# Modulation sums as rows in column quarters, layer norm factors by tokens, and low-rank products spread over row groups

## The chip, the core and the metric

The kernel runs on one core of one Trainium2 chip. The metric is the device time of one execution in microseconds (us); smaller is better. Five engines work side by side, each with a queue of its own: TensorE (PE, matrix products into the PSUM banks), VectorE (DVE), ScalarE (ACT), GpSimd (POOL) and SyncE (SP, which here only issues transfers). They wait for each other by semaphores.

## What is computed

Two transformer-like blocks of two layers each work on 512 tokens of width 1024, all in float32. The first has a recurrent or a forgetting-attention mixer, cross-attention to 256 memory tokens and a squared-ReLU MLP. The second is the one that the change touches most:

```python
for l in range(DEPTH):                                   # second_block
    mod = c_act @ ada_w[l] + ada_b[l]                    # 6144 numbers: six vectors of 1024
    sh1, sc1, gt1, sh2, sc2, gt2 = [m[:, None, :] for m in jnp.split(mod, 6, axis=-1)]
    h = rms_norm_2(x, norm1_g[l]) * (1 + sc1) + sh1
    if l == 0:
        p = h @ w_in[0]; vl = None
    else:
        p = h @ jnp.concatenate([w_in[l], v_down[l - 1]], axis=1)
        vl = token_shift(p[..., N_IN:], mu_v[l - 1])     # 32 wide
    ps = token_shift(p[..., :N_SHIFT], mu_shift[l])      # r, k, v, wl (64), al (64), gl (160)
...
    log_w = -jax.nn.softplus(-(w0 + jnp.tanh(wl) @ w_up)) - 0.5
    a = jax.nn.sigmoid(a0 + al @ a_up)
    g = jax.nn.sigmoid(gl) @ g_up
    v = v + (v_first - v) * jax.nn.sigmoid(v0 + vl @ v_up)   # layer 1 only
```

Then come the delta-rule scan, a pooling branch (trailing means over 2, 4, 8 and 16 frames and a linear map), two gated projections, an output product and a gated MLP.

## The kernel before

**Tiles.** The activations stay in SBUF as `xT`, 8 tiles of 128 features by 512 tokens. Each weight arrives in slabs of 1024 x 256 (1 MB) through two buffers `raw`. ACT rounds a slab to `whi` (line 858) and DVE writes the rest `wlo` (line 1533), both in a two-place ring. A product with the split operands takes three float32r matmuls (lines 2393 to 2395): high by high, high by low, low by high. One block of 128 output features is 8 x 3 of them, and a slab has two blocks. A matmul with plain float32 operands appears in the trace as two instructions.

**Order.** Every engine's program is written out by hand. `Plan.walk` numbers all PSUM results ("jobs"). Job j uses bank j mod 8, and PE may start it only when job j - 8 has been read (`bank_read`). The vectors in small tables (`vec`) come from `vrows` by a transpose on PE.

**Modulation.** While the first block's two MLPs run, POOL loads `ada_w` and DVE sums it into `ada_acc` (128 partial sums for each of 6144 columns; lines 1967 and 1970). PE then adds up the 128 partitions: 48 products with a 128 x 128 piece of `ada_acc` as the stationary operand and one column of ones moving. For layer 0 these stand between the matmuls of a slab (`adaln_beside`, line 2612, slab `v`,0 of the first block's layer 1). For layer 1 they stand in a row (`adaln(1)`, line 2491), ahead of the first product `lat` of the second block. `adaln` on DVE (lines 1624 to 1634) puts the result into `mod` and derived tables.

**Front norms** (before `lat`, numbers 4 and 6 in the code). ACT squares the 8 tiles (line 888), DVE adds them up (1544, 1547), and PE multiplies by a matrix of 1/1024 (`mean_square`, 2474), which gives the mean square in all partitions. ACT takes the root of 128 x 512 (893) and DVE the reciprocal (1552). Then for each tile DVE scales (1566), ACT shifts and rounds to `hh` (900), and DVE makes `hl` (1573), on which `lat`'s matmuls wait tile by tile. For norm 6 (layer 1) the squares are made beside the last products of layer 0; for norm 4 they all come after the first block's last MLP product.

**Low-rank part.** After `lat` (two blocks: 64 + 64 features for wl and al, 128 of gl) comes `gl1` (a block with 32 useful features, the rest of gl), in layer 1 also `vl` (another block with 32), then the slab `k2`,0. Then PE makes `lw` (4 products of 64 rows, partitions 0 to 63; line 2779), `la` (4 of 64 rows, partitions 64 to 127; 2782) and in layer 1 `lv` (4 of 32 rows, all on partitions 0 to 31; 2787), then slab `k2`,1. ACT reads them by sigmoids (1260). A shifted result is made by ACT (1230, own share) and DVE (2018, the token before).

**Gates.** After the scan, PE makes for each t of 4 a product of 128 rows (3095) and one of 32 rows (3096, all on partitions 0 to 31) into one bank. DVE multiplies (2249), and ACT and DVE split the result. Then PE has the slab `g1` (48 matmuls) and four products `pool` (3109), each of which waits for POOL's window means of that tile (lines 806 to 815).

## Time and profile before

| | |
|---|---|
| median of 3 runs | 2894.18 us (2889.81 to 2898.56) |
| the profiled execution, its own time | 2896.48 us |
| its span in the trace | 2894.9 us |
| PE busy | 2758.8 us, 95% of the span |
| DVE, ACT, POOL busy | 1601.4, 987.7, 211.2 us |
| matmuls of lines 2393 to 2395 with `hh` and `mh` | 2040 + 1248 of each line |

In the profile a busy PE isn't always at full speed. The granted clock (PEclk) of a stretch tells which of two levels, 2.4 GHz (1.00) or 1.2 GHz (0.50), it had. A matmul shown as 0.39 us long starts 0.23 us after the one ahead of it at the full clock, and at half the clock 0.43 us after it. The chain of work that ended last says which instruction was waited for at each moment, so the times between the starts are what counts.

### The profile page before, as it was taken

The numbers are of one execution on the slowest core, as the hardware profiler recorded it, in microseconds if no ns is written. First come the engines' busy times: TensorE is split into PE (matmuls) and PEld (weight loads), VectorE is DVE, ScalarE is ACT, GpSimd is POOL, SyncE is SP. The second block draws the span as 40 slices with busy tenths as digits, with TensorE's granted clock in tenths as the row PEclk, the third lists the DMA queues.
The fourth block names the chain that finished last, engine by engine and source line by source line (L and its number), as shares of the span: only waits on it lengthen the run. The fifth ranks groups of instructions, "written<-read, shape, count | busy, mean of one in ns | idle before, by whom it ended". The sixth has DMA issues, their size and how long they took to land.

```text
span 2894.9 us, 45409 instructions
## 1 busy us (share of the span) xinstructions
PE 2758.8 (95%) x19273; PEld 2287.6 (79%) x19273; DVE 1601.4 (55%) x2301; ACT 987.7 (34%) x1352; POOL 211.2 (7%) x268
## 2 busy tenths in 40 slices
PE   8989999999999999998999999999878899999998
PEld 6778888898688888767868788888667868888887
DVE  5657777755677777564453553334485454543334
ACT  5643212334532122343333331223433333432223
POOL 4100000000000000001040000000020040000000
PEclk9999999999999999899999999999899999999999
DMA  4234555512045555120022323232210022323322
GB/s 152 90 107 128 182 167 166 165 59 73 17 140 178 171 166 171 55 74 25 4 78 88 102 88 102 91 99 82 73 59 12 3 87 89 101 90 100 101 89 72
DMA packets 238530, 281.94 MB, mean 97 GB/s; under 512 B 7444, under 2 KB 224856, under 8 KB 238344
## 3 DMA queue, kind: packets, MB, share of 16 engines
q1 hardware_dynamic: 225312, 227.07, 24.7%
q0 software_dynamic: 12896, 52.11, 6.1%
q8 instruction: 148, 2.42, 0.4%
q14 instruction: 38, 0.31, 0.0%
q10 hardware_dynamic: 136, 0.03, 0.0%
HBM read 277.09 MB, written 2.10 MB: 96 GB/s over the span
## 4 chain that ended last, share of the span: by engine, by line
PE 87%; DVE 7%; ACT 4%; issue 2%; DMA 1%; ACTq 0%; DVEq 0%; POOL 0%; POOLq 0%
PE psum L2393 24%; PE psum L2394 24%; PE psum L2395 24%; DVE wlo L1533 2%; PE psum L2452 1%; ACT whi L858 1%; PE psum L2894 1%; PE psum L2453 1%; PE psum L2454 1%; PE psum L2909 1%; PE psum L2491 1%; PE psum L2877 1%; PE psum L2824 1%; PE psum L3010 0%; PE psum L3016 0%
## 5 line engine op out<-in xcount | busy, mean ns | idle before, releaser
L1533 DVE TENSOR_TENSOR wlo<-raw,whi 128x2048 fp32r<-128x2048 f32 x222 | 520.7, 2346 | 529.7 <-ACT whi L858 529.4
L2393 PE MATMUL psum<-hh,whi 128*128 128x512 f32 (+1 forms) x2040 | 792.2, 388 | 19.6 <-DVE hl L1573 6.6
L2394 PE MATMUL psum<-hl,whi 128*128 128x512 f32 (+1 forms) x2040 | 785.5, 385 | 0.0
L2395 PE MATMUL psum<-hh,wlo 128*128 128x512 f32 (+1 forms) x2040 | 784.5, 385 | 0.0
L858 ACT ACTIVATE whi<-raw 128x2048 fp32r<-128x2048 f32 x222 | 423.9, 1909 | 558.7 <-PE psum L2395 554.6
L2393 PE MATMUL psum<-mh,whi 128*128 128x512 f32 (+1 forms) x1248 | 486.4, 390 | 3.1 <-issue 2.3
L2394 PE MATMUL psum<-ml,whi 128*128 128x512 f32 (+1 forms) x1248 | 480.1, 385 | 0.0
L2395 PE MATMUL psum<-mh,wlo 128*128 128x512 f32 (+1 forms) x1248 | 479.9, 385 | 0.0
L2393 PEld LDWEIGHTS psum<-hh,whi 128*128 128x128 f32 x2040 | 386.7, 190 | 109.1 <-issue 26.8
L2395 PEld LDWEIGHTS psum<-hh,wlo 128*128 128x128 f32 x2040 | 386.4, 189 | 76.1
L2394 PEld LDWEIGHTS psum<-hl,whi 128*128 128x128 f32 x2040 | 386.7, 190 | 74.6 <-issue 0.5
L2393 PEld LDWEIGHTS psum<-mh,whi 128*128 128x128 f32 x1248 | 235.7, 189 | 48.9 <-issue 4.5
L2395 PEld LDWEIGHTS psum<-mh,wlo 128*128 128x128 f32 x1248 | 235.4, 189 | 46.4
L2394 PEld LDWEIGHTS psum<-ml,whi 128*128 128x128 f32 x1248 | 235.5, 189 | 44.3 <-issue 0.5
L1970 DVE SCALAR_TENSOR_TENSOR rest<-rest,cact 128x192 f32<-128x192 f32 (+1 forms) x448 | 187.7, 419 | 15.8
L1677 DVE SCALAR_TENSOR_TENSOR xT<-psum,mod,xT 128x512 f32<-128x512 f32 x64 | 47.4, 750 | 156.5 <-PE psum L2395 156.5
L1211 ACT ACTIVATE mh<-rest 128x512 fp32r<-128x512 f32 x64 | 40.5, 633 | 253.1 <-DVE rest L1981 253.1
L798 POOL DMA_DIRECT2D rest<-in_ada_w x64 | 56.7, 887 | 922.7 <-DVE rest L1970 618.8
L1675 DVE TENSOR_TENSOR xT<-xT,psum 128x512 f32<-128x512 f32 x80 | 54.6, 685 | 110.2 <-PE psum L2395 110.2
L2340 DVE TENSOR_TENSOR rest<-rest,psum 128x512 f32<-128x512 f32 x40 | 27.5, 688 | 110.4 <-PE psum L2395 110.4
L1491 ACT ACTIVATE mh<-rest 128x512 fp32r<-128x512 f32 x44 | 27.8, 633 | 173.9 <-DVE rest L2340 172.5
L1484 ACT ACTIVATE rest<-psum 128x512 f32<-128x512 f32 x40 | 23.9, 598 | 143.3 <-PE psum L2395 143.2
(455 smaller groups left out, 2816.2 us busy)
## 6 DMA issues: line engine op xcount, KB each, us to landing
rest<-in_ada_w POOLq DMA_DIRECT2D x64, 768.0 KB, 5.3
raw<-in_w_gu SPq DMA_DIRECT2D x44, 1024.0 KB, 5.1
raw<-in_w_in SPq DMA_DIRECT2D x34, 1024.0 KB, 5.3
raw<-in_w_mlp_in SPq DMA_DIRECT2D x32, 1024.0 KB, 5.4
raw<-in_w_mlp_out SPq DMA_DIRECT2D x32, 1024.0 KB, 5.2
raw<-in_w_out SPq DMA_DIRECT2D x16, 1024.0 KB, 5.2
raw<-in_w_down SPq DMA_DIRECT2D x16, 1024.0 KB, 5.3
raw<-in_w_mem_kv SPq DMA_DIRECT2D x8, 1024.0 KB, 5.2
```

What stands on the lines that cost most here:

```text
L798: pool.dma_start(ada[:, s % 2, :, :], w[:, :, bass.ds(c * (per * ADA_COLS) + s * ADA_COLS, ADA_COLS)])\
L858: act.activation(whi[:, g % 2, :, :], raw[:, g % 2, :, :], ACT.Copy).then_inc(hi_done, 1)
L1211: act.activation(mh[:, m, :], f_t[:, m % 2, :], ACT.Square).then_inc(hid_hi, 1)
L1533: ins = dve.tensor_tensor(wlo[:, g % 2, :, :], raw[:, g % 2, :, :], f32(whi[:, g % 2, :, :]), ALU.subtract)
L1675: free(dve.tensor_tensor(xT[:, t, :], xT[:, t, :], bank(j), ALU.add), j)
L1677: free(dve.scalar_tensor_tensor(xT[:, t, :], bank(j), gate, xT[:, t, :], ALU.mult, ALU.add), j)
L1970: ins = dve.scalar_tensor_tensor(acc, w, cact[:, k:k + 1], acc, ALU.mult, ALU.add)
L2393: pe.matmul(out, whi_, xhi, start=first, stop=False)
L2394: pe.matmul(out, whi_, xlo, start=False, stop=False)
L2395: return pe.matmul(out, wlo_, xhi, start=False, stop=last)
L2452: pe.matmul(p[:, 0:n], xh[:, k, t], wh, start=(k == 0), stop=False)
L2453: pe.matmul(p[:, 0:n], xl[:, k, t], wh, start=False, stop=False)
```

## The change

- The modulation sums are turned round. `modulation_rows` makes three PSUM banks, each by four products: a column of ones, repeated 32 times, is stationary (128 x 32), and 512 columns of `ada_acc` move. Each product writes another quarter of the bank's partitions (32 equal rows). ACT copies a bank to SBUF (`modulation_row`, 128 x 512). `modulation_turned` brings the numbers from rows back to columns, by 4 products a bank with four columns of the identity matrix moving.
- For layer 0 the rows come after the slab `v`,0 and the turning after slab `k`,0, and nothing stands between the matmuls any more. For layer 1 the rows come right behind the last MLP product of the first block, ahead of the mean square. One bank is turned between the mean square and the factors, two behind the factors.
- The front norms take their mean squares by tokens (`mean_square_tokens`: 4 products of one column), root and reciprocal on 128 x 4, and spread the factor by 4 products with the identity (`factor_rows`). DVE's scaling reads it from PSUM. Norm 4's squares and sums move beside the last MLP products, as norm 6's already were.
- `gl1` and `vl` become one block. The 32 columns of the weights (and in layer 1 the 32 of `v_down`) are copied side by side four (two) times into 128 columns by the splitting itself (`latent_parts`), so that the 32 rows exist in every row group where they are wanted. The biases and loads of `mu_shift`, `mu_v`, `v_up` and `g_up` follow.
- `lw` and `la` alternate. `lv` runs on partitions 32 to 63 and 96 to 127 in turn. The four gate products of 128 rows come first, then the four of 32 rows, on four row groups in layer 0 and on two in layer 1.
- ACT takes a root of a small table at the start of the last `fd` slabs, which loads the function table there.

The diff, cut to its core:

```diff
@@ Plan.walk
                 self.slab_jobs("v", 1, 0, NT)
+                for r in range(3):
+                    self.add("mr", 0, r)
+                self.slab_jobs("k", 1, 0, NT)
                 self.add("mod", 0)
-                self.slab_jobs("k", 1, 0, NT)
...
-            if l:
-                self.lin("vl", l, 1, 1)
@@ vector (norm)
-                q.mark(dve.reciprocal(n_rstd, n_rs))
...
+                dve.reciprocal(tk[:, 1, :], tk[:, 0, :]).then_inc(S("front_factor"), 1)
+                j = J["rb", ni]
+                ready(dve, j)
+                norm_apply(ni, gain, shift, factor=bank(j))
@@ vector (last MLP chunk)
-                        if l == 0 and cc == CHUNKS1 - 1 and i >= 5:
-                            raw_lo(2, lambda t: V("norm_mix", 8 + t), (2 * i - 10, 2 * i - 9))
-                            norm_sums(2, range(max(1, 2 * i - 10), 2 * i - 8))
+                        if cc == CHUNKS1 - 1 and i >= 5:
+                            if l == 0:
+                                raw_lo(2, lambda t: V("norm_mix", 8 + t), (2 * i - 10, 2 * i - 9))
+                            norm_sums(2 + 2 * l, range(max(1, 2 * i - 10), 2 * i - 8))
@@ tensor
-                for n in range(48):
-                    ins = pe.matmul(p[:, n:n + 1], ada_acc[:, n * P:(n + 1) * P], ones[:, 0:1], start=True, stop=True)
+                for r in range(3):
+                    p = start("mr", l, r)
+                    for c in range(4):
+                        ins = pe.matmul(p[32 * c:32 * c + 32, :], ones[:, 0:1].to_broadcast([P, 32]),
+                                        ada_acc[:, (4 * r + c) * T:(4 * r + c + 1) * T], start=True, stop=True)
+                    done(ins)
...
+                evacuated(pe, J["mr", l, r])
+                for i in range(4):
+                    ins = pe.matmul(p[:, 16 * r + i:16 * r + 16:4], ada_rows[l][:, r, i * P:(i + 1) * P], ident[:, 0:P:32],
+                                    start=True, stop=True)
...
-                    linear_tokens("v", l, 0, h, NT, beside=adaln_beside)
...
+                    linear_tokens("v", l, 0, h, NT)
+                    modulation_rows(0)
...
-                mean_square(4 + 2 * l)
                 if l == 0:
-                    adaln(1)
+                    modulation_rows(1)
+                mean_square_tokens(4 + 2 * l)
+                if l == 0:
+                    modulation_turned(1, 0, ahead("mod", 1))
+                factor_rows(4 + 2 * l, l + 1)
...
                 linear("gl1", l, 0, h, blocks=1)
-                if l:
-                    linear("vl", l, 0, h, blocks=1)
...
-                        done(pe.matmul(p, VU[0:32, t * P:(t + 1) * P], VL[0:32, :], start=True, stop=True))
+                for t in range(4) if l else ():
+                    a = value_rows(t)
+                    p = start("lv", l, t)
+                    done(pe.matmul(p, VU[a, t * P:(t + 1) * P], GL[a, 1, :], start=True, stop=True))
...
+                p = [start("g", l, t) for t in range(4)]
                 for t in range(4):
-                    gate(t)
+                    pe.matmul(p[t], GU[:, 0, t * P:(t + 1) * P], GL[:, 0, :], start=True, stop=False)
+                for t in range(4):
+                    a = gate_rows(l, t)
+                    done(pe.matmul(p[t], GU[a, 1, t * P:(t + 1) * P], GL[a, 1, :], start=False, stop=True))
```

TensorE where the second block begins, before: the last MLP matmuls, then the mean square of norm 4, the 48 products of `adaln(1)`, then `lat`.

```order
4276 L2394 MATMUL psum<-ml,whi 128x512
4277 L2395 MATMUL psum<-mh,wlo 128x512
4278 L2474 MATMUL psum<-rest,mean_all 128x512
4279 L2491 MATMUL psum<-ones,rest 128x1 x48
4280 L2393 MATMUL psum<-hh,whi 128x512
```

The same place in the changed program (`rest` beside `ones` is `ada_acc`, beside `mean_all` the sum of squares, beside `ident` the copied rows; `tk` holds the factors).

```order
4254 L2452 MATMUL psum<-ml,whi 128x512
4255 L2453 MATMUL psum<-mh,wlo 128x512
4256 L2550 MATMUL psum<-rest,ones 32x512 x12
4257 L2567 MATMUL psum<-mean_all,rest 128x1 x4
4258 L2558 MATMUL psum<-ident,rest 128x4 x4
4259 L2575 MATMUL psum<-ident,tk 128x128 x4
4260 L2558 MATMUL psum<-ident,rest 128x4 x8
4261 L2451 MATMUL psum<-hh,whi 128x512
```

The sums of the modulation moved from behind the mean square to ahead of it, and 12 + 12 products stand for 48.

TensorE between slab `k2`,0 and slab `k2`,1 of the second block's layer 1, before: `lw`, `la`, `lv`.

```order
7611 L2395 MATMUL psum<-hh,wlo 128x512
7612 L2779 MATMUL psum<-rest 128x512 x4
7613 L2782 MATMUL psum<-rest 128x512 x4
7614 L2787 MATMUL psum<-rest 128x512 x4
7615 L2393 MATMUL psum<-hh,whi 128x512
```

And after, where L2862 is `lw`, L2864 is `la` and L2868 is `lv`.

```order
7570 L2862 MATMUL psum<-rest 128x512
7571 L2864 MATMUL psum<-rest 128x512
7572 L2862 MATMUL psum<-rest 128x512
7573 L2864 MATMUL psum<-rest 128x512
7574 L2862 MATMUL psum<-rest 128x512
7575 L2864 MATMUL psum<-rest 128x512
7576 L2862 MATMUL psum<-rest 128x512
7577 L2864 MATMUL psum<-rest 128x512
7578 L2868 MATMUL psum<-rest 128x512 x4
```

`lw` and `la` now take turns; `lv` keeps its place behind them and changes only its partitions.

## Rows read from the trace of the kernel before

**Rows 1.** The page: the chain that ended last, by line.
```profile
PE psum L2393 24%; PE psum L2394 24%; PE psum L2395 24%; DVE wlo L1533 2%; PE psum L2452 1%; ACT whi L858 1%; PE psum L2894 1%; PE psum L2453 1%; PE psum L2454 1%; PE psum L2909 1%; PE psum L2491 1%; PE psum L2877 1%; PE psum L2824 1%; PE psum L3010 0%; PE psum L3016 0%
```

**Rows 2.** The chain where the second block begins: start us, us, what.
```profile
1175.62 0.24 PE psum L2395
...
1182.01 2.08 PE psum L2474 x2
1184.08 20.27 PE psum L2491 x96
```

**Rows 3.** Stretches: busy us and counts, PEclk is the granted clock.
```profile
core 0: us, PE busy (x) PEld busy (x) DVE busy (x) ACT busy (x) POOL busy (x), PEclk, DMA share, GB/s
607.00:626.80 19.80, 19.80 (x172) 19.80 (x172) 2.73 (x15) 1.42 (x3) 0.00 (x0) 0.98 0.16 52
...
1182.00:1204.30 22.30, 22.29 (x99) 21.26 (x99) 14.23 (x17) 8.20 (x10) 0.00 (x0) 0.50 0.00 1
1204.30:1208.70 4.40, 4.40 (x12) 3.49 (x12) 3.08 (x8) 0.00 (x0) 1.07 (x2) 0.53 0.17 61
...
2080.30:2085.50 5.20, 5.20 (x10) 1.71 (x9) 0.00 (x0) 3.55 (x6) 0.00 (x0) 0.69 0.64 202
```

**Rows 4.** Instructions in order of time, norm 4: start us, us, engine, line.
```profile
1188.23 1.42 DVE L1566 SCALAR_TENSOR_TENSOR rest<-xT,gmod,rest 128x512 f32<-128x512 f32 x2
...
1197.73 1.63 DVE L1573 SCALAR_TENSOR_TENSOR hl<-rest,mod,hh 128x512 fp32r<-128x512 f32 x2
```

**Rows 5.** The same view, norm 6 and the start of `lat` in layer 1.
```profile
2027.80 3.07 DVE L1547 TENSOR_TENSOR rest<-rest 128x512 f32<-128x512 f32 x4
...
2030.93 1.99 PE L2474 MATMUL psum<-rest,mean_all 128*128 128x512 f32 x2 [3.83 <-DVE rest L1547]
...
2037.06 1.42 DVE L1566 SCALAR_TENSOR_TENSOR rest<-xT,gmod,rest 128x512 f32<-128x512 f32 x2
```

**Rows 6.** The same view, small products of TensorE elsewhere, and a small reciprocal.
```profile
1261.08 1.06 PE L2794 MATMUL psum<-mo,hsum 128*32 128x512 f32 x8
...
1477.58 1.14 PE L2800 MATMUL psum<-rest,hexp 32*128 32x512 f32 x8 [1.81 <-DVE rest L2235]
...
2885.43 1.05 PE L3167 MATMUL psum<-mean_all,rest 128*128 128x1 f32 x8 [2.08 <-DVE rest L1547]
...
2886.82 0.18 DVE L2367 RECIPROCAL tk<-tk 128x4 f32<-128x4 f32 x1 [1.44 <-ACT tk L1507]
...
32.33 2.07 PE L2544 MATMUL psum<-ident,tk 128*128 128x128 f32 x8 [3.91 <-DVE tk L1710]
```

**Rows 7.** The same view, TensorE behind slab `k`,0 of the first block.
```profile
640.78 0.67 PE L2484 MATMUL psum<-mo,mean 128*128 128x256 f32 x2 [0.92 <-DVE mod L1624]
```

**Rows 8.** The same view, ACT at `gl1` and `vl`, layer 1.
```profile
2058.59 0.68 ACT L1230 ACTIVATE rest<-psum,omm 32x512 f32<-32x512 f32 x1 [2.95 <-PE psum L2395]
...
2064.03 0.68 ACT L1230 ACTIVATE rest<-psum,omm 32x512 f32<-32x512 f32 x1 [2.96 <-PE psum L2395]
```

**Rows 9.** The same view, `lw`, `la` (layer 0), `lv` and the sigmoids (layer 1).
```profile
1233.60 2.41 PE L2779 MATMUL psum<-rest 64*128 64x512 f32 x5
...
1236.82 2.31 PE L2782 MATMUL psum<-rest 64*128 64x512 f32 x5
...
2077.29 4.72 ACT L1260 ACTIVATE mo<-psum,vec 128x512 f32<-128x512 f32 x8
...
2080.25 5.25 PE L2787 MATMUL psum<-rest 32*128 32x512 f32 x8
```

**Rows 10.** The same view, gates, window means and pooling products, layer 0.
```profile
1478.65 1.12 PE L3095 MATMUL psum<-rest 128*128 128x512 f32 x2
1479.70 1.12 PE L3096 MATMUL psum<-rest 32*128 32x512 f32 x2
...
1497.87 1.27 POOL L815 TENSOR_TENSOR rest<-mo,rest 128x512 f32<-128x512 f32 x1
...
1498.13 3.59 PE L3109 MATMUL psum<-rest 128*128 128x512 f32 x8
```

More of the change, by code:

```diff
@@ L201, in walk @@
         for l in range(2):
+            for r in range(3) if l == 0 else ():
+                self.add("mr", 1, r)
             self.add("ms", 4 + 2 * l)
+            self.add("rb", 4 + 2 * l)
             if l == 0:
@@ L579, in x_ready, with latent_parts @@
                 evacuated(eng, J["fd", ((ver - 6) // 2, len(CHUNKS2) - 1), t // 2, t % 2])
+        latents = {plan.slab["gl1", l, 0]: l for l in range(2)}
+        def latent_parts(dst, src, g):
+            n = 64 if latents[g] else 32
+            x = src[:, g % 2, :, 0:n].rearrange("p k (a b) -> p k a b", a=1).to_broadcast([P, KT, P // n, n])
+            return dst[:, g % 2, :, 0:P].rearrange("p k (a b) -> p k a b", b=n), x
         def bc(m, n=4):
@@ L888, in norm_squares, with modulation_row, root_tokens @@
                     act.activation(n_sq[:, t % 3, :], xT[:, t, :], ACT.Square).then_inc(S("norm_sq"), 1)
+            def modulation_row(l, r):
+                j = J["mr", l, r]
+                ready(act, j)
+                free(act.activation(ada_rows[l][:, r, :], bank(j), ACT.Copy), j)
+            def root_tokens(ni):
+                j = J["ms", ni]
+                ready(act, j)
+                free(act.activation(tk[:, 0, :], bank(j)[:, 0:NT], ACT.Sqrt, bias=epst[:, 0:1]), j)
             def norm_root(ni):
@@ L1497, in _ @@
                         hi(plan.slab["fd", (l, c), i] + 1)
+                        if c == 2 and i == 0:
+                            act.activation(rtok[:, 1, :], rtok[:, 1, :], ACT.Sqrt)
                         if c == 2 and i:
@@ L1547, in norm_sums, with norm, norm_apply @@
                         dve.tensor_tensor(n_acc, n_acc, n_sq[:, t % 3, :], ALU.add).then_inc(S("norm_added"), 1)
-            def norm(ni, gain, shift=None, slab=None):
+            def norm(ni, gain, shift=None):
                 evacuated(dve, J["ms", ni])
-                q.mark(dve.reciprocal(n_rstd, n_rs))
-                if slab is not None:
-                    lo(slab)
-                q.settle()
-                norm_apply(ni, gain, shift)
-            def norm_apply(ni, gain, shift=None, between=None):
+                dve.reciprocal(tk[:, 1, :], tk[:, 0, :]).then_inc(S("front_factor"), 1)
+                j = J["rb", ni]
+                ready(dve, j)
+                norm_apply(ni, gain, shift, factor=bank(j))
+                dve.wait_ge(S("norm_lo"), 8 * ni + KT)
+                dve.sem_inc(bank_read[j % BANKS], 1)
+            def norm_apply(ni, gain, shift=None, between=None, factor=n_rstd):
                 for t in range(KT + 1):
@@ L2602, in _ @@
                     done(ins)
-                    mods = bank(J["mod", 0])
-                    def adaln_beside(b, k):
-                        if (b, k) == (1, 0):
-                            ahead("mod", 0)
-                            pe.wait_ge(ada_done, 256 + 16)
-                        for n in range(16 * b + 2 * k - 16, 16 * b + 2 * k - 14) if b else ():
-                            ins = pe.matmul(mods[:, n:n + 1], ada_acc[:, n * P:(n + 1) * P], ones[:, 0:1], start=True, stop=True)
-                        return ins if b else None
-                    linear_tokens("v", l, 0, h, NT, beside=adaln_beside)
-                    start("mod", 0)
-                    done(pe.matmul(mods[:, 47:48], ada_acc[:, 47 * P:48 * P], ones[:, 0:1], start=True, stop=True))
+                    linear_tokens("v", l, 0, h, NT)
+                    modulation_rows(0)
                     linear_tokens("k", l, 0, h, NT)
+                    p = start("mod", 0)
+                    for r in range(3):
+                        ins = modulation_turned(0, r, p)
+                    done(ins)
                     head_means(1, 0, mean_128, m_sq1, MEM)
@@ L3089, in _ @@
                 pe.wait_ge(S("gate_latent"), 2 * l + 2)
-                pe.wait_ge(s_lora, small + 48)
-                def gate(t):
-                    p = start("g", l, t)
-                    pe.matmul(p, GU[:, 0, t * P:(t + 1) * P], GL[:, 0, :], start=True, stop=False)
-                    done(pe.matmul(p, GU[0:32, 1, t * P:(t + 1) * P], GL[0:32, 1, :], start=False, stop=True))
+                pe.wait_ge(s_lora, small + 96)
                 pe.wait_ge(S("gn_inv"), l + 1)
```

123 lines of the change are left out of this document (80 added, 43 removed), and 2 rows, old and new, of the table tiles.

## The prediction, made before the changed kernel ran

> **What bounds the kernel now.** I read the chain that ended last first: the three lines of the split product, 2393 to 2395, are 72% of it, and their counterparts follow [rows 1]. TensorE is the path nearly everywhere, so an edit counts by what it takes out of TensorE's row of instructions, or by how long TensorE stands still. Three kinds of places matter. At the start of the second block TensorE ends the MLP at 1175.86, waits for the norm's sums until 1182.01, and then works off 96 light instructions in 20.27 us, so that `lat` starts at 1204.35 [rows 2]. The norm itself was finished by 1199.4 [rows 4]; the modulation is what `lat` waits for. The stretches [rows 3] show why it is dear: the clock is at 1.2 GHz (0.50) all through it, and it comes back only 4.4 us into `lat`. In slab `v`,0 of the first block 96 such instructions stand between slab matmuls at 0.98 [rows 3]. And there are the small f32 products of the low-rank part and the gates [rows 9, 10].
>
> **Paces used.** A block of 24 matmuls takes 2064.03 - 2058.59 = 5.44 us at the full clock, 0.227 each [rows 8]; with 256 columns I take 0.12. At half the clock 12 matmuls take 4.4 us instead of 2.7 [rows 3]. An f32 instruction of 512 columns follows its like by 0.43 [rows 9, 10]. Four products of 128x32 in four column quarters take 1.06 together, and four of 32 rows in four row groups 1.14 [rows 6].
>
> **Part A, modulation of layer 0.** The stretch of 19.8 us holds 172 instructions [rows 3]: 76 slab matmuls (9.1 us), so the 96 others cost 10.7 us, 0.11 each. They go, and so does the wait of 0.92 us behind slab `k`,0, where the fourth product takes the bank that DVE frees only with `mod` [rows 7]; that bank is another job's now. New on the path: three banks of rows, 3 x 1.06 = 3.2 us, and 24 turning instructions at 0.11, 2.6 us. ACT's three copies lie beside slab `k`,0 (96 matmuls, 11.5 us). DVE's `adaln(0)` waits for a later job now, but its successors are counted from the same point and keep up. Gain 11.6 - 5.8 = **5.8**. The bounds of the rows are 1.06 a bank from the nearest row, and 4 x 0.86 = 3.4 if the four ran one by one (eight instructions of 0.43) [rows 10].
>
> **Part B, start of the second block.** The rows need only `ada_acc`, which is complete, so they run from 1175.86 to 1179.1 while DVE still adds. Four of seven sums are left behind the last addition; one takes 0.79 (3.07 for four, less the last) [rows 5], so the mean square starts 3 x 0.79 = 2.4 us earlier, at 1179.6. From its start to the end of the reciprocal on 128x4 the last norm of the kernel needs 2887.00 - 2885.43 = 1.57 us [rows 6]: 1181.2. The first bank's turning (8 instructions, 0.9) lies in that gap. Factors: 8 instructions, 0.9 us at the full clock, 2.07 at half [rows 6]. I take full: scaling starts at 1182.3. Scale, shift, and remainder of the first tile are about 0.75 each [rows 4], so `lat` starts at 1184.7; the other 16 turning instructions (1.8 us) are done by 1184.3. Gain 1204.35 - 1184.7 = **19.7**. TensorE has had 5 us of light work by then, and light work did not bring the clock back in 22 us [rows 3], so I expect `lat` to start at half the clock again, as before. If it stays up, 1.7 more. `lat` can't then end before DVE does, 11.1 us from first scaling to last remainder [rows 4], about what its 48 matmuls take. What is late next is DVE with `adaln(1)` and `gl1`'s remainder, half as long as before; it fits.
>
> **Part C, `lw` and `la`, layer 0.** 16 instructions from 1233.60 to 1239.1, 5.5 us: five of one row group alone, some together, then five of the other alone [rows 9]. Taking turns, each group has 8 x 0.43 = 3.4, 3.6 with the start. Gain **1.9**; 0 if nothing more overlaps, and -1.4 if what overlaps now is lost (16 x 0.43).
>
> **Part D, gates, layer 0.** A pair of 128 rows and the pair of 32 follow each other at 1.05 us [rows 10], 8.4 for eight pairs. Now 8 x 0.43 + 1.14 = 4.6, plus a little for the change of groups, so TensorE reaches the pooling products 3.7 us earlier, at 1494.6. But the fourth of these needs POOL's last window means, ready at 1499.14 whatever TensorE does [rows 10]. It then ends at 1500.1 instead of 1501.7. Gain **1.6**, not 3.7. VectorE's split of the gated values has g1's 11 us as its cover.
>
> The Trainium skill (TensorEngine Tiling (Array Packing), Key Properties) says that changing the tiling mode, not just the tile, drains TensorE. The row agrees: a mixed pair costs 1.05 against 0.86 for the unmixed. The rule would add such a drain around each new group of quarter products; by the rows that is 0.2 us for some eight places, 1.5 us off the sum, or nothing where the rows of 1.06 and 1.14 hold it already, as I assume.
>
> **Part E, norm 6 in layer 1.** The mean square starts at 2030.93 and scaling at 2037.06 [rows 5], 6.13 us. Now: 8 instructions at half the clock, 1.7 (the pace of line 2491, 0.21), 0.7 for root and reciprocal, 2.07 for the factors [rows 6]: 4.5. Gain **1.7**; at the full clock 3.6.
>
> **Part F, `vl`.** One block less, **5.4** us of TensorE [rows 8]. Its slab's rounding and remainder were ACT's and DVE's idle time. `k2`,0 then follows `gl1` directly, as in layer 0, where nearly nothing waits.
>
> **Part G, `lw`, `la`, `lv`, layer 1.** Before 5.5 + 5.2 = 10.7, with a clock that falls to half during `lv` (0.69 on average) [rows 3, 9]. After: 3.6 for the first two, and two streams of four for `lv`. Each `lv` bank must first be emptied by ACT's sigmoids (0.59 each, starting 2.4 us in) [rows 9]: the fourth at 4.9 us, so the end is 5.9. Gain 4.8, and 1.5 for a clock that stays up: **6.3**. The skill's same page (PSUM Bottleneck) warns that after a speedup of TensorE the emptying of PSUM may bind. By TensorE alone the end would be 5.5, by the sigmoids 5.9; the sum has the latter.
>
> **Part H, gates, layer 1.** Two row groups: 3.4 + 1.9. POOL's last tile binds as in layer 0. Gain **1.5**.
>
> At nothing: the five extra small loads on SP at the start (the slab behind them is needed 30 us later), POOL's extra six loads (hundreds of us ahead of their use), the squares and sums beside the last MLP products, the extra sigmoid of 0.6, the wait for `v_down`'s load. Each is under cover of TensorE's slab matmuls; uncovered, each would cost 1 to 3 us. The early load of the root's table lies beside slabs, and no root waits for it now either.
>
> **Sum.** 5.8 + 19.7 + 1.9 + 1.6 + 1.7 + 5.4 + 6.3 + 1.5 = 43.9 us. Against the profiled execution (2896.5) that is 2852.6; it stood 2.3 above the median, so against 2894.2 the forecast is **2850.3**.
>
> **Rivals.**
> *Clock up at the second block.* TensorE never stands still for more than about 1 us there, which speaks for it; the 22 us at 0.50 speak against. With Part E at the full clock: 1.7 + 1.9 more, 2846.7. Chance 0.2.
> *Quarters don't overlap.* Each product of rows has other moving data, as at line 2794, which overlaps [rows 6]. If it fails: 24 x 0.86 = 20.6 instead of 6.4, 14 us back in A and B, and 2864.5. Chance 0.06.
> *Row groups gain little in C and G.* The present overlap of two groups might be all there is: 1.9 + 1.9 + 2.6 + 1.5 lost, 2858. Chance 0.12.
> *A new wait of its own.* The factor bank, the copies of `gl1` or DVE's later `adaln(0)` might bind: 4 to 8 us, 2856. Chance 0.12.
> *The windows don't bind*, because POOL is freed of some contention: at most 3.5 us more, 2846.8. Chance 0.03.
> *Slower.* One mechanism: the rows in quarters run one by one at half the clock, each with its weight load in front. A full f32 product at half the clock takes 2.08 us [rows 2]. With 0.5 for an exposed load, an estimate, 24 products take 62 us instead of 6.4, 56 us back: 2906. It decides from 2.1 us a product (43.9 / 24 + 0.27). The row at 1.06 for four speaks against. Chance 0.01.
>
> **How the numbers follow.** Forecast 0.46, the rest as given. The range reaches from 2844 (clock up) to 2862, and leaves out the serial quarters, the slower case and the ends of the others. A measurement of this kernel can tell about 0.3%, 8.7 us, from no change. Faster by more than that holds in all cases but the slower one and an unseen mishap: 0.97, same 0.02, slower 0.01.
>
> **What would show it.** Each bank of rows takes about 1.1 us. `lat` of layer 0 starts 9 us behind the last MLP matmul instead of 28.5; PEclk there is near 0.5 for about 4 us. Line 2612's work is gone from `v`,0. `lw` and `la` take 3.6 us. No fall of the clock at `lv`. TensorE waits for POOL about 1.5 us before the fourth pooling product, twice. The forecast is wrong if the rows take 3.4 us a bank, if `lat` waits for anything but its first tile, or if a DVE wait appears behind slab `k`,0.

## The result, and the profile after

| | time, us | runs |
|---|---|---|
| before | 2891.99 median (2888.96 to 2898.56) | 4 |
| after | 2857.99 median (2856.42 to 2859.57) | 4 |
| ratio | 0.9878, 95% interval 0.9861 to 0.9895 | |
| profiled execution | 2859.57, span 2857.8 (before 2896.48, span 2894.9) | |

The change takes 34.0 us off the median, and 37.1 us off the span between the two traces. The forecast was 2850.3 in a range of 2844 to 2862, from a sum of 43.9 us. So the time is inside the range, and 7.7 us above the forecast. The forecast started from 2894.2, the median of three runs of before; a fourth run makes it 2891.99, so by the medians the gain is 9.9 us under the sum. The traces, 37.1, are 6.8 under it.

The page of after, the chain that ended last, by line (it answers to [rows 1]):

```profile
PE psum L2451 24%; PE psum L2453 24%; PE psum L2452 24%; DVE wlo L1594 1%; PE psum L2510 1%; PE psum L2975 1%; POOL mo L838 1%; PE psum L2990 1%; PE psum L2512 1%; PE psum L2511 1%; ACT whi L893 1%; PE psum L2958 1%; PE psum L2905 1%; POOL mo L839 0%; PE psum L3091 0%
```

The split product (now lines 2451 to 2453) still holds 72%. The line of the one-column products is gone from the list, and GpSimd's window sums (L838, L839) are new in it.

The second block's start in after, instructions in order of time (start us, us, engine, line; it answers to [rows 2, 4]). The last MLP product starts at 1171.94.

```profile
1172.26 2.78 PE L2550 MATMUL psum<-rest,ones 128*32 128x512 f32 x24
...
1172.97 3.07 DVE L1608 TENSOR_TENSOR rest<-rest 128x512 f32<-128x512 f32 x4
...
1176.10 1.05 PE L2567 MATMUL psum<-mean_all,rest 128*128 128x1 f32 x8 [1.05 <-DVE rest L1608]
1177.01 1.03 PE L2558 MATMUL psum<-ident,rest 128*128 128x4 f32 x8
...
1177.48 0.18 DVE L1613 RECIPROCAL tk<-tk 128x4 f32<-128x4 f32 x1 [1.44 <-ACT tk L935]
1177.90 1.66 PE L2575 MATMUL psum<-ident,tk 128*128 128x128 f32 x8
1179.36 3.41 PE L2558 MATMUL psum<-ident,rest 128*128 128x4 f32 x16
1179.60 1.41 DVE L1628 SCALAR_TENSOR_TENSOR rest<-xT,gmod,psum 128x512 f32<-128x512 f32 x2 [1.94 <-PE psum L2575]
...
1181.14 0.75 DVE L1635 SCALAR_TENSOR_TENSOR hl<-rest,mod,hh 128x512 fp32r<-128x512 f32 x1
...
1182.63 0.77 PE L2451 MATMUL psum<-hh,whi 128*128 128x512 f32 x1
```

The last line is the start of `lat`, 1182.63, 10.69 us after the start of the last MLP product; in before it was 1204.22 - 1175.46 = 28.76. The twelve quarter products take 2.78 us together. The last 16 turning instructions take 3.41 us, about twice the 0.11 each of the forecast, and VectorE had the first tile's remainder ready at 1181.89 (L1635), 0.7 us before `lat`.

The same places as stretches of after (columns as in [rows 3]; the fourth number from the right is the granted clock):

```profile
core 0: us, PE busy (x) PEld busy (x) DVE busy (x) ACT busy (x) POOL busy (x), PEclk, DMA share, GB/s
616.60:619.40 2.80, 2.80 (x26) 0.76 (x25) 0.00 (x0) 1.67 (x3) 0.00 (x0) 1.00 0.03 6
...
1171.90:1182.60 10.70, 9.64 (x66) 7.19 (x66) 6.41 (x11) 3.75 (x8) 0.00 (x0) 0.80 0.01 2
1182.60:1187.00 4.40, 4.40 (x11) 3.48 (x12) 4.40 (x7) 2.60 (x4) 1.07 (x2) 0.50 0.21 60
2049.70:2055.60 5.90, 5.90 (x26) 4.03 (x25) 1.26 (x1) 5.88 (x11) 0.00 (x0) 1.00 0.59 188
```

The third data line is the start of `lat`: 0.50, that is 1.2 GHz, as in before. The fourth is `lv` and what follows: the clock no longer falls there (0.69 before, [rows 3]).

The decay products and `lv` of layer 1 in after (it answers to [rows 9]), then the gates of layer 0 and 1 and the end of layer 0's pooling products (it answers to [rows 10]):

```profile
2046.04 0.69 PE L2862 MATMUL psum<-rest 64*128 64x512 f32 x1
2046.05 0.69 PE L2864 MATMUL psum<-rest 64*128 64x512 f32 x1
...
2049.15 0.59 PE L2862 MATMUL psum<-rest 64*128 64x512 f32 x1
2049.16 0.59 PE L2864 MATMUL psum<-rest 64*128 64x512 f32 x1
...
2049.68 2.45 PE L2868 MATMUL psum<-rest 32*128 32x512 f32 x8
```

```profile
1458.00 5.40 PE L3177 MATMUL psum<-rest 128*128 128x512 f32 x8
1463.33 1.14 PE L3180 MATMUL psum<-rest 32*128 32x512 f32 x8
...
1475.43 2.73 PE L3188 MATMUL psum<-rest 128*128 128x512 f32 x6
...
1479.00 1.13 PE L3188 MATMUL psum<-rest 128*128 128x512 f32 x2 [0.84 <-POOL rest L843]
...
2297.91 3.70 PE L3177 MATMUL psum<-rest 128*128 128x512 f32 x8
2301.54 1.99 PE L3180 MATMUL psum<-rest 32*128 32x512 f32 x8
...
2319.64 1.12 PE L3188 MATMUL psum<-rest 128*128 128x512 f32 x2 [2.42 <-POOL rest L843]
```

The two row groups' products start 0.01 us apart and a pair takes 0.43. The small gates overlap four deep in layer 0 (1.14) and two deep in layer 1 (1.99). The fourth pooling product waits for GpSimd, 0.84 us in layer 0 and 2.42 in layer 1 (forecast: about 1.5 in both).

### The profile page after: what moved, and what is told of

The parts are those of the page before. It is cut to its first block, busy times and chain, and to the rows that moved or that the text cites. A ratio compares the mean times of both kernels' runs of the same rounds, so it can differ in the third digit from the quotient of the medians.

```text
span 2857.8 us, 45255 instructions
## 1 busy us (share of the span) xinstructions
PE 2728.9 (95%) x19179; PEld 2265.0 (79%) x19179; DVE 1588.9 (56%) x2299; ACT 987.8 (35%) x1359; POOL 216.5 (8%) x277
## 4 chain that ended last, share of the span: by engine, by line
PE 86%; DVE 6%; ACT 3%; POOL 2%; issue 2%; DMA 0%; ACTq 0%; DVEq 0%; POOLq 0%
PE psum L2451 24%; PE psum L2453 24%; PE psum L2452 24%; DVE wlo L1594 1%; PE psum L2510 1%; PE psum L2975 1%; POOL mo L838 1%; PE psum L2990 1%; PE psum L2512 1%; PE psum L2511 1%; ACT whi L893 1%; PE psum L2958 1%; PE psum L2905 1%; POOL mo L839 0%; PE psum L3091 0%
## 5 line engine op out<-in xcount | busy, mean ns | idle before, releaser
L1594 DVE TENSOR_TENSOR wlo<-raw,whi 128x2048 fp32r<-128x2048 f32 x219 | 513.2, 2344 | 519.6 <-ACT whi L893 519.2
L2398 DVE TENSOR_TENSOR rest<-rest,psum 128x512 f32<-128x512 f32 x40 | 27.5, 687 | 110.4 <-PE psum L2453 110.4
```

The lines of the kernel that those rows point to most:

```text
L1594: ins = dve.tensor_tensor(wlo[:, g % 2, :, :], raw[:, g % 2, :, :], f32(whi[:, g % 2, :, :]), ALU.subtract)
```

## A table by stage

VectorE's remainders of the slabs are marks that every kernel has in the same order. The table gives what lies between the starts of two of them, in us, from each kernel's trace: slabs 0 to 3 (the start-up), 16 to 56 (first block, layer 1, where modulation 0 is), 56 to 59 (that layer's attention), then `lat`'s start after the start of the last MLP product, and the gates with the pooling of both layers (105 to 107, 169 to 172, without the slab `vl` of before). The number behind the slash is the mean granted clock.

| kernel | start-up | 16 to 56 | attention | to `lat` | gates 0 | gates 1 | span |
|---|---|---|---|---|---|---|---|
| before | 34.4 | 460.5 | 117.65 / 0.97 | 28.76 | 33.3 | 38.2 | 2894.9 |
| after | 34.6 | 454.2 | 120.07 / 0.94 | 10.69 | 32.3 | 37.3 | 2857.8 |
| after_again | 34.6 | 454.2 | 120.12 / 0.94 | 10.74 | 31.9 | 37.4 | 2858.2 |
| after_timed | 34.8 | 453.1 | 118.48 / 0.96 | 9.76 | 32.5 | 38.9 | 2850.6 |
| cols_layer0 | 32.0 | 459.3 | 117.65 / 0.97 | 9.76 | 32.4 | 37.2 | 2854.9 |
| cols_layer1 | 33.5 | 454.6 | 120.19 / 0.94 | 28.80 | 32.4 | 37.2 | 2875.5 |
| pairs_order | 33.5 | 454.2 | 120.05 / 0.94 | 10.70 | 42.4 | 39.9 | 2873.5 |
| squares_behind | 33.5 | 454.3 | 120.10 / 0.94 | 15.10 | 32.4 | 37.2 | 2860.7 |
| filler_one | 34.9 | 459.0 | 117.63 / 0.97 | 11.19 | 33.0 | 36.3 | 2861.0 |
| no_windows_before | 33.5 | 459.3 | 117.66 / 0.97 | | 32.5 | 37.4 | 2886.2 |
| no_windows_after | 34.3 | 454.0 | 121.19 / 0.93 | | 28.8 | 34.5 | 2850.3 |
| pool_late | 34.4 | 454.1 | 119.91 / 0.94 | 10.14 | | | 2850.4 |
| pool_late_cols0 | 34.7 | 459.5 | 119.93 / 0.94 | 10.15 | | | 2858.6 |

Read it down a column: where a column's instructions are the same, its spread is what the clock does by itself. Where the clock was 1.00 throughout, the stretches repeat: slabs 59 to 70 take 121.88 to 121.92 us in all thirteen traces.

## Experiments

### The same kernel again

Nothing edited.

> The changed kernel once more, nothing edited, for a second trace. In the first, the changed kernel gained 37.1 us of span instead of the 43.9 forecast; 2.4 of the shortfall fell in the attention of the first block's layer 1 (from the product of its values to its end, 707 to 779 us of before) and 1.9 in the scan of the second block's layer 0, with the same waits and a lower granted clock there. Theory A (the clock's loss is by where the fall happens to lie): those two stretches come out at another length in this trace, by up to 2 us each, and length and mean granted clock of the stretch go together. Theory B (the edits put a fixed cost there): both stretches repeat within 0.3 us. Front norm 4, the alternating decay products and the gates repeat within 0.3 us under both.

Measured: span 2858.2, and the attention 120.12 at 0.94: a repeat within 0.1 us, against theory A as it was put. The scan (62.3 for 62.6) and the gates of layer 0 (31.9 for 32.3) moved by 0.4 to 0.5, a little more than the 0.3 expected. But after_timed (below), the same kernel again, has 118.48 at 0.96, its start of `lat` at 9.76 instead of 10.7, and a span of 2850.6. So one kernel does vary by 7 us between executions, in stretches whose clock varies with them; that two executions agreed was no proof. Theory B's fixed cost falls with that.

### Layer 0's modulation by columns

```
-                    linear_tokens("v", l, 0, h, NT)
-                    modulation_rows(0)
...
+                    linear_tokens("v", l, 0, h, NT, beside=adaln_beside)
+                    start("mod", 0)
+                    done(pe.matmul(mods[:, 47:48], ada_acc[:, 47 * P:48 * P], ones[:, 0:1], start=True, stop=True))
                     linear_tokens("k", l, 0, h, NT)
-                    p = start("mod", 0)
-                    for r in range(3):
-                        ins = modulation_turned(0, r, p)
-                    done(ins)
```

> The changed kernel with only layer 0's modulation taken back: 48 one-column products beside the value projection in place of 3 quarter-row banks and 12 turning products. By the forecast's part A the stretch from the first block's second value slab to the attention loses 5.8 us (5.94 measured between the traces). Theory A (clock by position): the attention behind it, shifted by that, takes between the 71.5 us of before and the 73.9 of after, and its clock follows. Theory B (another edit costs 2.4 us there): it stays at 73.9 us. The rest of the kernel keeps its lengths within 1 us a stretch; the span 5 to 8 us above after.

Measured: slabs 16 to 56 take 459.3 instead of 454.2, so Part A is worth 5.1 us there (6.3 between before and after, and 6.2 against after_timed, 453.1). The 1.2 us between after and after_timed lie in the one stretch 52 to 53, 18.4 us at a granted clock of 0.87 and 17.3 at 0.91, so the edit can't be priced closer than 5.1 to 6.3. The attention behind it takes 117.65 instead of 120.07, as in before. The span expectation missed: 2854.9 is 2.9 below after, since the start-up (2.6), the slabs 7 to 16 (119.2 for 120.8), the attention (2.4) and the start of `lat` (0.9) all came out shorter, and nothing was edited in any of them. Timed against each other with the later kernels (pool_late and pool_late_cols0) the columns cost 8.2 us in the traces and 6.5 in the medians, 2859.54 against 2853.07: the sign of the single pair of traces was the clock's. The long attention also comes with the columns (pool_late_cols0, 119.93).

The attention as stretches, of after_timed, cols_layer0 and filler_one in turn (columns as above):

```profile
657.25:775.73 118.48, 107.43 (x807) 88.89 (x807) 69.40 (x200) 68.90 (x200) 0.00 (x0) 0.96 0.09 28
```
```profile
660.48:778.13 117.65, 106.48 (x807) 87.89 (x807) 69.14 (x199) 68.48 (x200) 0.00 (x0) 0.97 0.09 28
```
```profile
663.30:780.93 117.63, 106.22 (x807) 87.80 (x807) 69.22 (x200) 68.41 (x200) 0.00 (x0) 0.97 0.09 28
```

The same 807 products; VectorE and ScalarE are as busy in each. Only TensorE's busy time and clock differ.

### Layer 1's modulation by columns

```
-                    modulation_rows(1)
                 mean_square_tokens(4 + 2 * l)
...
-                    modulation_turned(1, 0, ahead("mod", 1))
                 factor_rows(4 + 2 * l, l + 1)
...
-                    modulation_turned(1, 1, p)
-                    done(modulation_turned(1, 2, p))
...
+                    for n in range(48):
+                        ins = pe.matmul(p[:, n:n + 1], ada_acc[:, n * P:(n + 1) * P], ones[:, 0:1], start=True, stop=True)
+                    done(ins)
```

> The changed kernel with only layer 1's modulation as 48 one-column products, put behind the factor rows; norm 4 by tokens and its early squares stay. Before, those products took 20.3 us (96 records). Forecast's reasoning: they are on the path here, and replace 3.2 us of turning behind the factors and 0.9 before them, so the latent product starts 16 to 17 us later after the last MLP product than in after (10.4 us): 26.5 to 27.5. Rival (they were slow only through the clock, or part of them hides behind the scaling of the input on VectorE, 2 to 3 us): 22 to 25.

Measured: `lat` starts 28.80 us after the last MLP product, 18.1 later than in after, 1.3 above the expected 26.5 to 27.5 and equal to before (28.76). In order of time:

```profile
1173.69 1.86 PE L2561 MATMUL psum<-mean_all,rest 128*128 128x1 f32 x8 [3.77 <-DVE rest L1602]
1176.12 2.08 PE L2569 MATMUL psum<-ident,tk 128*128 128x128 f32 x8 [0.56 <-DVE tk L1607]
1177.99 20.48 PE L2843 MATMUL psum<-ones,rest 128*128 128x1 f32 x96
```

The norm by tokens and its early squares, alone, bring nothing here: what they take off ahead of the columns they put back as factor rows on TensorE, and the columns take 20.5 us either way. So the gain of the place hangs on the modulation. That is its form and its place together: the columns stand behind the norm here, the rows in after stand ahead of it, right behind the MLP. What the 48 columns would take in that place no run shows.

### Squares behind the MLP

```
-                            if i >= 5:
-                                norm_squares(2 + 2 * l, (2 * i - 10, 2 * i - 9))
+                            if l == 0 and i >= 5:
+                                norm_squares(2, (2 * i - 10, 2 * i - 9))
```

with ScalarE's other squares and VectorE's sums of norm 4 moved in the same way.

> The changed kernel with only norm 4's squares and sums moved back behind the MLP; the quarter rows and the norm by tokens stay. Mean square came 6.6 us after the last MLP product in before and 4.2 in after. Forecast's reasoning (the norm's chain is what the latent product waits for, once the modulation is short): the latent product starts 12.5 to 13.5 us after the last MLP product, where after has 10.7. Rival (the turning products hide it): under 11.2.

Measured: 15.10 us, later than either theory. The mean square came at 6.55 instead of 4.16, the expected 2.4. The other 2.0 us are clock: TensorE waited 3.45 us instead of 1.05 in front of it, and then every light instruction ran at half the pace.

```profile
1177.37 1.87 PE L2569 MATMUL psum<-mean_all,rest 128*128 128x1 f32 x8 [3.45 <-DVE rest L1609]
1179.09 1.85 PE L2560 MATMUL psum<-ident,rest 128*128 128x4 f32 x8
1180.80 2.05 PE L2577 MATMUL psum<-ident,tk 128*128 128x128 f32 x8
1182.65 3.41 PE L2560 MATMUL psum<-ident,rest 128*128 128x4 f32 x16
```

So with the rows in place the early squares are worth 4.4 us. Ahead of the columns, together with the norm by tokens, they are worth nothing (cols_layer1).

### The order of the small products

```
-                for t in range(4):
-                    pe.matmul(p[t], GU[:, 0, t * P:(t + 1) * P], GL[:, 0, :], start=True, stop=False)
                 for t in range(4):
+                    p = start("g", l, t)
+                    pe.matmul(p, GU[:, 0, t * P:(t + 1) * P], GL[:, 0, :], start=True, stop=False)
                     a = gate_rows(l, t)
...
```

and `lw` four times, then `la` four times, on all engines.

> The changed kernel with the row groups and the copied rows kept, but the order of the small products of before: four decay products, then four of the rates; and each gate's two products together. Forecast's reasoning (two row groups run side by side only when neighbours in the queue): layer 0's eight products take 8 x about 0.4 us again instead of about 1.7 in all, so both layers' second key slab starts 1.7 to 1.9 us later; the gates' last product 2 to 3.5 us later, but the pooling products, which wait for GpSimd's windows, no more than 1 us later. Rival (the tile position alone brings the gain, not the order): all within 0.3 us of after.

Measured: the decay products cost 1.82 us more in layer 0 (slabs 96 to 99: 40.30 for 38.48) and 1.35 more in layer 1's stretch. Layer 0 is as the forecast's reasoning says, layer 1 falls short of the 1.7 expected (its four `lv` products spread over 1.40 us from first to last start there, in after over 1.86); the rival falls. The gates missed by far: 10.0 us more in layer 0 and 2.6 in layer 1, where at most 1 was expected. In order of time, a pair in layer 0 and a pair in layer 1:

```profile
1462.20 2.07 PE L3180 MATMUL psum<-rest 32*128 32x512 f32 x2
...
1464.20 2.08 PE L3178 MATMUL psum<-rest 128*128 128x512 f32 x2
...
2315.23 1.12 PE L3180 MATMUL psum<-rest 32*128 32x512 f32 x2
...
2316.28 1.13 PE L3178 MATMUL psum<-rest 128*128 128x512 f32 x2
```

```profile
1455.20:1472.30 17.10, 17.06 (x25) 4.31 (x25) 8.19 (x11) 1.89 (x3) 15.53 (x22) 0.54 0.00 0
```

In layer 0 the clock fell behind the factor rows and stayed at half through nearly all eight products: 1.0 us a record instead of 0.53. In before the same order ran there at the full clock [rows 10]. From the first start to the last end the eight take 15.97 us here and 8.46 in before, so 7.5 us are the clock in the same order. In after's order they take 4.77 at the full clock (cols_layer0) and 6.47 in after, where it was low for part of them, so the order is worth 3.7 at the full clock, as forecast. Then the slab `g1` begins at the low clock too, and the pooling products start 13.2 us behind the gates instead of 11.0. The pairwise order does not always meet a half clock, and what decides whether it falls there stays open.

### The windows left out, in both kernels

GpSimd's window sums and means are left out, and one scaling of each tile stands in their place, so these two kernels compute other values.

```
-                    while step < w:
+                    while step < 1:
...
-                    q.step(pool.tensor_scalar(cur[:, 16:T], cur[:, 16:T], 1.0 / w, None, ALU.mult))
-                    pool.tensor_tensor(Z[t], cur.rearrange("p (a b) -> p a b", a=4), Z[t], ALU.subtract)...
+                    pool.tensor_scalar(Z[t], Z[t], 1.0 / w, None, ALU.mult)...
```

> The changed kernel with the pooling left out: GpSimd's window sums and means (40 instructions in each layer) are replaced by one scaling of each of the four tiles, so the pooling products read other values. Forecast's reasoning (part D: the gates' products end 3.7 us earlier, GpSimd's windows let only 1 to 1.6 of that through): with the windows gone the last pooling product follows the gate projection without a wait, and the stretch from the gate slab to the second slab behind it (32.3 us in layer 0 of after, 37.3 for three slabs in layer 1) shortens by 0.9 to 2 us. Rival (the projection itself, not the windows, sets the start): under 0.3 us.

> The kernel before with the same part left out. There the pooling products began at 1498.13 us, 0.26 after the last window. Forecast's reasoning: the projection ends there at about the same time as the windows, so without the windows the stretch (33.3 us in layer 0, 38.2 in layer 1) shortens by under 0.5 us, and the two kernels without windows differ by about 2.5 to 3.7 us in each layer, where with them they differ by 1.0 and 0.9. Rival: both shorten alike and the difference stays at 1.

Measured: after shortens by 3.6 us in layer 0 and 2.7 in layer 1, where 0.9 to 2 was expected; before by 0.8 and 0.7, where under 0.5 was. Both ran these stretches at a clock of 1.00. Without windows the kernels differ by 32.48 - 28.76 = 3.7 us in layer 0 and 37.44 - 34.54 = 2.9 in layer 1, with them by 1.0 and 0.9. The gates' gain is what the forecast worked out (3.7), and the windows hide about 70% of it. The pooling products of after without windows, in order of time, stand behind the projection without a gap:

```profile
1460.09 1.14 PE L3177 MATMUL psum<-rest 32*128 32x512 f32 x8
...
1472.17 3.59 PE L3185 MATMUL psum<-rest 128*128 128x512 f32 x8
1475.20 0.79 PE L2448 MATMUL psum<-mh,whi 128*128 128x512 f32 x1
```

### Filler ahead of the attention

```
-                    for r in range(3):
+                    for r in 2 * (0, 1, 2):
                         ins = modulation_turned(0, r, p)
```

> The changed kernel with the 12 turning products of layer 0's modulation issued twice (the same values written again): 2.6 us more work on TensorE about 30 us ahead of the attention. Between traces so far the attention stretch (slab 56 to 59) has only two lengths: 117.7 us at a granted clock of 0.97 where the modulation is by columns (before, cols_layer0), 120.1 at 0.94 where it is by rows (after, twice, and two variants). Theory A (it depends on where in time the clock falls): the stretch takes another length than 120.1, between 117.5 and 122, and the span does not grow by exactly 2.6. Theory B (the row form itself costs 2.4 us there): 120.1 again, and 2.6 us in all.

Measured: the attention takes 117.63 at 0.97, with the row form in place: theory B falls, the row form costs nothing there. The 24 light instructions more did not cost 2.6 us but 6.0 in the slabs 53 to 56, where they stand (44.46 for 38.51), since the clock fell there (0.92, in after 1.00). Part of that can be the clock's own, for cols_layer1 has 40.16 there without any filler. Slabs 16 to 56 show only 4.8 of it (459.0 for 454.2), because the stretch 52 to 53 had the shorter of its two lengths, as in after_timed. The attention was 2.4 shorter. The span grew by 3.2.

### Two moves more, timed

```
-                for t in range(4) if b == 0 else (): ... start("pool", l, t) ...
                 linear("pa", (l, b), 0, y, K=4, ...)
+                for t in range(4) if b == 0 else (): ... start("pool", l, t) ...
```

```
                     modulation_rows(1)
+                    modulation_turned(1, 0, ahead("mod", 1))
                 mean_square_tokens(4 + 2 * l)
                 if l == 0:
-                    modulation_turned(1, 0, ahead("mod", 1))
+                    modulation_turned(1, 1, ahead("mod", 1))
                 factor_rows(4 + 2 * l, l + 1)
```

> The changed kernel, timed in five rounds beside the two below on the same chip. Both theories expect a ratio to before of 0.986 to 0.990.

> The changed kernel with two more moves. The four pooling products of each layer go behind the first output projection's slab (VectorE and ScalarE take their share in the same order), so that GpSimd's windows no longer stand ahead of it; and at the second block's start modulation quarters 0 and 1 are turned before and behind the mean square, so only quarter 2 stands behind the factor rows. Forecast's reasoning (windows hide 2.7 of the gates' 3.7 us): gate slab to second slab behind 29 to 31 us in layer 0 instead of 32.3, three slabs 34.5 to 36 in layer 1 instead of 37.3; latent product 9.6 to 10.1 us after the last MLP product instead of 10.7; together 3.5 to 6 us, from which the clock can take or to which it can add 2 to 3 us somewhere else. Rival (a new wait for the pooled tiles ahead of the second projection takes the gain back): within 1 us of after in both layers.

> The same with layer 0's modulation by columns, as in cols_layer0, whose single look was 3.2 us shorter than after although its own stretch was 5.1 longer. Theory A (where the clock falls is fixed by the program, and moves with small edits): the attention takes 117.7 us or another of the lengths seen, the start-up stretch 32 to 34.6, and the span lies within 4 us of pool_late, on either side. Theory B (layer 0's rows are worth 5 us in the end): 4 to 6 us longer than pool_late.

Measured, four runs each, on one chip beside before at 2891.3:

| | median, us | ratio to before | 95% interval |
|---|---|---|---|
| after_timed | 2856.55 | 0.9878 | 0.9861 to 0.9894 |
| pool_late | 2853.07 | 0.9859 | 0.9839 to 0.9879 |
| pool_late_cols0 | 2859.54 | 0.9884 | 0.9865 to 0.9903 |

pool_late's pooling products in layer 0, in order of time:

```profile
1475.41 1.28 POOL L842 TENSOR_TENSOR rest<-mo,rest 128x512 f32<-128x512 f32 x1
...
1475.57 3.60 PE L3187 MATMUL psum<-rest 128*128 128x512 f32 x8
```

TensorE no longer waits for GpSimd. Since VectorE takes its slabs in another order now, the gates' stretch is not comparable to the table; from the gate slab to the end of all four groups (slabs 105 to 122) it is 152.3 us against 156.0 in layer 0, and 153.7 against 154.5 in layer 1 (169 to 186), where the clock fell once more. pool_late_cols0, with the same move, has 155.4 and 153.8; the seven traces with the gates of after and without the move have 154.7 to 159.1 and 154.5 to 156.2. So in layer 1 both are 0.7 us or more below all seven, and in layer 0 the clock moves the stretch by as much as the gain that was expected. `lat` starts 10.14 us after the last MLP product instead of 10.69, between the lengths that after itself has had (9.76 to 10.74); VectorE's first remainder is late now, TensorE waits 0.97 for it. The median is 3.5 us below after_timed, the low end of what was expected, and the intervals overlap: the gain of the two moves is not shown. Against pool_late, layer 0's columns are slower by 6.5 us in the medians (a little over theory B's 4 to 6) and by 5.4 in their own stretch, slabs 16 to 56, so Part A is real, though these intervals overlap as well.

## Why the prediction was right, point by point

The direction and the range held. The mechanisms of all eight parts are in the traces; the sum was 7 to 10 us too large. Parts A, B, C, D and H were also tried by experiments; E, F and G, 13.3 us, are read from the traces of before and after, with only the order of `lw` and `la` in G tried by itself.

- **Part A (5.8).** 6.3 us between the traces of before and after, 5.1 against cols_layer0, 5.4 between pool_late and pool_late_cols0. Rows overlap as assumed, 0.93 us a bank where 1.06 was taken.
- **Part B (19.7).** 18.1. The mean square came 3.84 us behind the rows' start, as worked out (1179.6 - 1175.86 = 3.7). The step that failed is "I take full" for the factors' clock: they took 1.66, and the 16 turning instructions behind them 3.41 instead of 1.8, at a clock that fell in the middle of the factors. Then the turning, not VectorE, released `lat`. In after_timed the clock fell later (factors 1.14, turning 2.96) and `lat` stood at 9.76. The step named the right two prices and chose the cheaper one; for the turning it had only one price. The forecast also put the place's gain down to several edits at once; cols_layer1 and squares_behind show that the norm's part has worth only with the short modulation.
- **Part C (1.9).** 1.83 (slabs 96 to 99, 40.31 to 38.48), and the same by pairs_order.
- **Parts D and H (1.6, 1.5).** 1.0 and 0.9. That GpSimd binds was right; that it ends at the same time was the small error: counted from the gate slab's remainder its last window of layer 0 ended at 28.58 us (1478.94 - 1450.36) instead of 28.17 (1499.14 - 1470.97). Part of the gates in layer 0 ran at half the clock (5.40 for eight instructions where 3.44 was taken), and GpSimd hid that too: in cols_layer0 the eight took 3.70, TensorE waited 2.54 us for the last window instead of 0.84, and the stretch was the same, 32.4. Unmasked, the gain is 3.7 and 2.9, the forecast's 3.7 and a little under the 3.1 by its working of layer 1.
- **Parts E, F, G (1.7 + 5.4 + 6.3 = 13.4).** Together 13.3, from the mean square of norm 6 to the first product behind `k2`,1 (78.20 us in before, 64.86 in after). E gave 1.6 (mean square to scaling 4.55 for 6.13), F 5.4, and G 4.6 up to the start of `k2`,1 (6.01 for 10.63) and 1.7 in that slab, where the clock stays up, as forecast.
- **At nothing.** No new wait appeared. What the forecast left out is not an edit's cost but the clock elsewhere: the attention of the first block lost 2.4 us, the scan of layer 0 about 1.8 (60.8 to 62.6 in slabs 104 to 105; 62.3 and 61.6 in the other two executions of after). The attention shows its short length with the rows (filler_one, 117.63) and its long one without them (pool_late_cols0, 119.93).

Put together: at their own places the parts gained 6.3 + 18.1 + 1.8 + 1.0 + 13.3 + 0.9 = 41.4 us. The clock took 2.4 in the attention, 1.8 in the scan and 0.8 more inside `lat`, and gave 1.6 in layer 1 (slabs 172 to 186, 117.27 for 118.84, two lengths of a stretch that nobody edited). That makes 38.0; the traces have 37.1, and the 0.9 between is spread in small pieces.

Of the rivals, none happened. "Row groups gain little in C and G" gave the nearest time, 2858, and is false: C and G gained 1.8 and 6.3. "A new wait of its own" gave 2856, also for a reason that is not there. A time near a rival's is no proof of it, and how well the sum came out is in part luck: what the clock did outside the edited places, 3.4 of the 6.8 us that are missing between the traces, was in no term of it, and it could as well have been less or more. The 0.5 us that the slower rival took for an exposed weight load is shown by no run; the rows took 0.93 a bank.

The Trainium skill (TensorE: Matmul & The Clock Gate, What's actually happening) says that the chip's watch on TensorE's activity runs freely and is not tied to the kernel's start, so that the place of a change of clock differs from run to run. The traces agree: one kernel, three executions, an attention of 120.07, 120.12 and 118.48 us, and `lat` at 10.69, 10.74 and 9.76.

The Trainium skill's rule on the drain when the tiling changes (TensorEngine Tiling (Array Packing), Key Properties) was left out of the sum. In layer 1 the eight full gate instructions and the change to the row groups take 2301.54 - 2297.91 = 3.63 us, against 8 x 0.43 = 3.44: about 0.2, half of it between the first two instructions (2297.91 and 2298.45) and half at the change itself. That is no more than the 0.2 that the prediction gave a place, and small beside the clock.

## What to carry to other kernels

Price light work on TensorE at both clocks and carry the two as a range, and look for it right behind a wait: a wait of 3.45 instead of 1.05 us cost 2.4 by itself and 2.0 more in the instructions behind it. When an engine is made faster ahead of a join, the other side of the join sets the gain; leave that side out once (here the windows, in both kernels) and the hidden part can be read. And where the clock moves a stretch that nobody edited by 1 to 3 us, compare stretches, not spans: the spans of one pair of traces had the sign of a 6 us edit wrong.

## What the runs showed of the hardware that was not expected

The clock's share differs between kernels in stretches that are the same in all of them and lie ahead of any edit: the start-up takes 32.0 us at 1.00 in cols_layer0, 33.5 at 0.95 in four others, 34.3 to 34.9 at 0.90 in the rest. In the three executions of after it stayed within 0.3 us. That would fit an influence of the kernel's build, but three executions of one build don't show it.

Filler of 24 light instructions cost 6.0 us in its stretch, not 2.6, since the clock fell there (0.92 for 1.00); without filler the same stretch has taken 38.5 to 40.2.

A copy of 128x2 values on GpSimd takes 0.53 us, and 2.13 when VectorE's remainder of a slab runs beside it (itself 3.05 instead of 2.29). In after, in order of time:

```profile
1450.36 3.05 DVE L1594 TENSOR_TENSOR wlo<-raw,whi 128x2048 fp32r<-128x2048 f32 x1 [11.83 <-ACT whi L893]
1451.33 2.13 POOL L839 COPY mo<-mo 128x2 f32<-128x2 f32 x1
...
1459.87 0.53 POOL L839 COPY mo<-mo 128x2 f32<-128x2 f32 x1
```

The Trainium skill (SBUF — State Buffer, Terms) calls the port pair that the two engines share an exclusive lock, held for the whole instruction; the copy that ends with the remainder (1453.46 and 1453.41) fits. The remainder's own 0.76 us more fits the lock as well: an add of GpSimd (1450.22 to 1451.26) was under way when it started. In after two of GpSimd's small copies took 2.13 and 2.14 us in the gates of layer 0, each beside a remainder, and in before two took 2.13. As an estimate that is about 3 us of GpSimd's chain (2.13 - 0.53 for each), more than the 0.84 us that TensorE waits for its end; no run took the remainders away.
